# Interleaved attention and expert choice: two projection halves cut into quarters, and the probability masks issued earlier on VectorE

## What is computed

```
h = rmsnorm(x) * (1 + scale) + shift
q, k, v = split(h @ w_qkv + b_qkv)                 # 16 query heads, 4 key heads, width 64
p = softmax(scores + relative bias, with a sink)   # window of 128 keys, blocks of 128 tokens
x = x + g_m * (p @ v @ w_o + b_o)                  # the second projection
h2 = rmsnorm(x) * (1 + scale_f) + shift_f
top_val, top_idx = top_k(h2 @ w_r + b_r, 4)        # choice of 4 of 32 experts
x = x + g_f * sum over chosen experts of gate * (swiglu(h2 @ w_in[e]) @ w_out[e])
out = rmsnorm(x)
```

## Time and profile before

| what | value |
|---|---|
| median of 3 runs | 1975.12 us (1974.99 to 1975.28) |
| profiled execution, its own time | 1975.76 us |
| its span, first to last instruction | 1974.3 us |
| mean granted TensorE clock | 0.993 of full |
| TensorE busy | 1928.8 us (98%) |
| VectorE busy | 654.8 us (33%) |
| ScalarE busy | 467.3 us (24%) |
| GpSimd busy | 217.4 us (11%) |
| second projection, TensorE (line 1502) | 256 instructions, 114.1 us |

### The profile page before, as it was taken

How to read it: one execution, slowest core, us unless ns; L and a number is a source line. 1 busy time by engine, 2 the same in 40 slices (tenths; PEclk the granted TensorE clock), 3 DMA queues, 4 the chain that set the end, 5 groups by cost and what they waited for, 6 DMA issues and landing times.

```text
span 1974.3 us, 50841 instructions
## 1 busy us (share of the span) xinstructions
PE 1928.8 (98%) x22939; PEld 1729.2 (88%) x22939; DVE 654.8 (33%) x1886; ACT 467.3 (24%) x1382; POOL 217.4 (11%) x250
## 2 busy tenths in 40 slices
PE   7999999988999999999999999999999999999997
PEld 4756755445999999999999999999999999999997
DVE  2645766565422222131222222222222222222224
ACT  3104544441121211111111111121211111112213
POOL 2003000001011011010111111111010101101002
PEclk9999999989999999999999999999999999999999
DMA  9880121114988888888888787979797999999986
GB/s 359 308 173 21 43 75 54 43 43 158 372 312 298 289 302 315 300 290 302 310 293 324 290 324 287 338 272 358 259 368 253 354 321 327 345 328 339 323 322 223
DMA packets 150208, 523.95 MB, mean 265 GB/s; under 512 B 10027, under 2 KB 15811, under 8 KB 149987
## 3 DMA queue, kind: packets, MB, share of 16 engines
q1 hardware_dynamic: 131186, 467.68, 65.8%
q0 software_dynamic: 17200, 52.59, 7.8%
q10 hardware_dynamic: 1600, 0.36, 0.1%
HBM read 485.34 MB, written 34.21 MB: 263 GB/s over the span
## 4 chain that ended last, share of the span: by engine, by line
PE 94%; DVE 2%; DMA 1%; SPq 1%; issue 1%; POOL 0%; ACT 0%; ACTq 0%; DVEq 0%; POOLq 0%
PE ps L1654 47%; PE ps L1688 24%; PE ps L1502 5%; PE ps L1451 4%; PE ps L1510 3%; PE ps L1642 2%; PE ps L1628 2%; PE ps L1429 2%; PE ps L1483 1%; PE ps L1447 1%; DMA ring<-in_w_qkv 1%; PE ps L1472 1%; SPq L417 0%; SPq L405 0%; DMA U<-xn_d,U 0%
## 5 line engine op out<-in xcount | busy, mean ns | idle before, releaser
L1654 PE MATMUL ps<-U,ring 128*64 128x120 f32 (+11 forms) x13312 | 935.4, 270 | 2.2 <-DMA ring<-in_moe_w 1.7
L1654 PEld LDWEIGHTS ps<-U,ring 128*64 128x64 f32 (+1 forms) x13312 | 922.9, 149 | 10.1 <-issue 8.5
L1688 PE MATMUL ps<-U,ring 128*64 128x120 f32 (+11 forms) x6656 | 469.3, 270 | 2.1 <-issue 1.7
L1688 PEld LDWEIGHTS ps<-U,ring 128*64 128x64 f32 (+1 forms) x6656 | 461.6, 149 | 6.7 <-issue 6.0
L1238 DVE TENSOR_SCALAR U<-ps,U 128x120 f32<-128x120 f32 (+11 forms) x256 | 90.8, 355 | 1092.4 <-PE ps L1654 1092.4
L816 ACT ACTIVATE U<-U 128x120 f32<-128x120 f32 (+11 forms) x256 | 80.2, 313 | 889.1 <-DVE U L1238 889.1
L827 ACT ACTIVATE U<-ps,U,modT 128x120 f32<-128x120 f32 (+11 forms) x256 | 118.8, 464 | 290.0 <-PE ps L1688 289.9
L580 POOL DMA_INDIRECT acc_d<-U x43 | 43.2, 1006 | 767.1 <-DVE U L1230 763.4
L1502 PE MATMUL ps<-ring 128*128 128x512 f32 x256 | 114.1, 599 | 0.0
L1502 PEld LDWEIGHTS ps<-ring 128*128 128x128 f32 x256 | 47.3, 190 | 59.2 <-issue 59.2
L802 ACT ACTIVATE U<-ps,modT,Af 128x120 f32<-128x120 f32 (+11 forms) x252 | 91.6, 468 | 10.0 <-PE ps L1628 10.0
(11 more groups left out here) (229 smaller groups left out, 1107.1 us busy)
## 6 DMA issues: line engine op xcount, KB each, us to landing
ring<-in_moe_w SPq DMA_DIRECT2D x191, 2048.0 KB, 9.7
U<-in_w_mod SPq DMA_DIRECT2D x8, 2048.0 KB, 13.1
ring<-in_w_mod SPq DMA_DIRECT2D x3, 2048.0 KB, 19.7
ring<-in_w_qkv SPq DMA_DIRECT2D x3, 2048.0 KB, 18.0
acc_d<-xr SPq DMA_DIRECT2D x10, 512.0 KB, 2.9
xr<-in_x SPq DMA_DIRECT2D x8, 512.0 KB, 9.5
ring<-in_w_o SPq DMA_DIRECT2D x2, 2048.0 KB, 8.4
xn_d<-U SPq DMA_DIRECT2D x8, 512.0 KB, 2.6
```

The costliest lines, as they stand in the source:

```text
L1654: last = pe.matmul(bank(j % 4)[lo:hi, s * 256:s * 256 + n], w[:, k, s, (j % 2) * P + lo:(j % 2) * P + hi], xT[:, k, 0:n], start=(k == 0), ...
L1688: last = pe.matmul(bank(m % 4)[lo:hi, 0:n], w[:, k, (m % 4) * P + lo:(m % 4) * P + hi], actT[:, k, 0:n], start=(k == 0), stop=(k == KT - 1))
```

## The change

The second projection of a tile whose follower starts more than two steps later runs in three parts in three steps: columns 0 to 511, 512 to 767 and 768 to 1023. These are tiles 5 and 6, counted from 0 (steps 26, 27, 28 and 29, 30, 31). Parts are numbered through from 0 to 17 and their banks alternate by that number; the last one still uses its own bank. Gates, residuals and the waits of ScalarE and SyncE count parts instead of halves. On VectorE, in the steps 19, 21 and 23 to 31, `probs_out(u)` is issued in step u, behind the places and ahead of the denominators of u+1 and of everything that waits for norm, list or logits; before, it was the first of step u+1.

```diff
@@ -331,7 +331,15 @@
             return max(2 * KT + 2 * t, 4 * (t + 1) + 1)
 
         q_late = {n: (n // 2, n % 2) for n in range(2 * KT)}
-        o_half = {o_start(t) + h: (t, h) for t in range(TT) for h in range(2)}
+        o_parts = []
+        for t in range(TT):
+            o_parts.append((o_start(t), t, 0, 512))
+            if t + 1 < TT and o_start(t + 1) > o_start(t) + 2:
+                o_parts += [(o_start(t) + 1, t, 512, 768), (o_start(t) + 2, t, 768, D)]
+            else:
+                o_parts.append((o_start(t) + 1, t, 512, D))
+        o_at = {part[0]: n for n, part in enumerate(o_parts)}
+        parts_to = [sum(part[1] <= t for part in o_parts) for t in range(TT)]
         normed = {o_start(t) + 3: t for t in range(TT)}
         x2_half = {o_start(t) + 4 + h: (t, h) for t in range(TT) for h in range(2) if (t, h) != (TT - 1, 1)}
         logit_at = {o_start(t) + 6: t for t in range(TT - 1)}
@@ -339,7 +347,7 @@
         rank_at = {o_start(t) + 7: t for t in range(TT)}
         place_at = {o_start(t) + 8: t for t in range(TT)}
         STEPS = o_start(TT - 1) + 10
-        summed_after = {u + 1: u for u in range(UNITS) if u and (u in choose_at or u in place_at or u in normed)}
+        waits_late = {u for u in range(1, UNITS) if u in choose_at or u in place_at or u in normed}
 
         def lists_before(t):
             return sum(u < o_start(t) + 6 for u in place_at)
@@ -353,8 +361,8 @@
         def choice_bank(t):
             return bank(0) if t == LAST else bank(3)
 
-        def o_bank(t, h):
-            return bank(1) if (t, h) == (LAST, 1) else bank(7 - 2 * h)
+        def o_bank(n):
+            return bank(1) if n == len(o_parts) - 1 else bank(7 - 2 * (n % 2))
 
         def q_bank(n):
             return bank(7 - 2 * (n % 2))
@@ -450,10 +458,10 @@
                 sp.dma_start(xn_d[t * P:(t + 1) * P, :], xn2[:, t % 2, :]).then_inc(s_xnd[t % 2], 16)
 
             def store_x1(t):
-                sp.wait_ge(s_x1, 2 * t + 2)
+                sp.wait_ge(s_x1, parts_to[t])
                 sp.dma_start(acc_d[t * P:(t + 1) * P, :], xr[:, t, :]).then_inc(s_x1d, 16)
 
-            sp.wait_ge(s_x1, 2)
+            sp.wait_ge(s_x1, parts_to[0])
             for b in range(2):
                 sp.dma_start(acc_d[SEQ + b * P:SEQ + (b + 1) * P, :], xr[:, 0, :]).then_inc(s_x1d, 16)
             for t in range(TT - 2):
@@ -754,7 +762,7 @@
                                bank(6)[:, 0:256].rearrange("p (m n) -> p m n", m=2), ACT.Copy).then_inc(s_at, 1)
 
             def squares2(t):
-                act.wait_ge(s_x1, 2 * t + 2)
+                act.wait_ge(s_x1, parts_to[t])
                 if t:
                     act.wait_ge(s_sq2, t)
                 act.activation(junk2, xr[:, t, :], ACT.Square, accum_out=ss[:, TT + t:TT + t + 1]).then_inc(s_sq2, 1)
@@ -1012,18 +1020,18 @@
                 link(dve.tensor_tensor(out=den[:, u % 2, :], in0=rs[:, u % 2, :], in1=es[:, u % 2, :], op=ALU.add))
                 dve.reciprocal(rec[:, u % 2, :], den[:, u % 2, :]).then_inc(s_rec, 1)
 
-            def o_gate(t, h):
-                cols = slice(h * 512, h * 512 + 512)
-                dve.wait_ge(s_op, 2 * t + h + 1)
-                if t or h:
-                    dve.wait_ge(s_x1, 2 * t + h)
-                dve.tensor_tensor(out=gated, in0=o_bank(t, h), in1=gmB[:, cols], op=ALU.mult).then_inc(s_gt, 1)
-
-            def residual(t, h):
-                cols = slice(h * 512, h * 512 + 512)
-                dve.wait_ge(s_gt, 2 * t + h + 1)
+            def o_gate(n):
+                _, t, lo, hi = o_parts[n]
+                dve.wait_ge(s_op, n + 1)
+                if n:
+                    dve.wait_ge(s_x1, n)
+                dve.tensor_tensor(out=gated[:, 0:hi - lo], in0=o_bank(n)[:, 0:hi - lo], in1=gmB[:, lo:hi], op=ALU.mult).then_inc(s_gt, 1)
+
+            def residual(n):
+                _, t, lo, hi = o_parts[n]
+                dve.wait_ge(s_gt, n + 1)
                 dve.wait_ge(s_xb, t + 1)
-                dve.tensor_tensor(out=xr[:, t, cols], in0=xr[:, t, cols], in1=gated, op=ALU.add).then_inc(s_x1, 1)
+                dve.tensor_tensor(out=xr[:, t, lo:hi], in0=xr[:, t, lo:hi], in1=gated[:, 0:hi - lo], op=ALU.add).then_inc(s_x1, 1)
 
             def norm2(t):
                 dve.wait_ge(s_rstd2, t + 1)
@@ -1094,19 +1102,21 @@
 
             scores_in(0)
             for u in range(STEPS):
-                if 1 <= u <= UNITS:
+                if 1 <= u <= UNITS and u - 1 not in waits_late:
                     probs_out(u - 1)
-                if u < UNITS and u not in summed_after:
+                if u < UNITS and u - 1 not in waits_late:
                     denominators(u)
                 if u + 1 < UNITS:
                     scores_in(u + 1)
-                if u - 1 in o_half:
-                    o_gate(*o_half[u - 1])
-                    residual(*o_half[u - 1])
+                if u - 1 in o_at:
+                    o_gate(o_at[u - 1])
+                    residual(o_at[u - 1])
                 if u in place_at:
                     places(place_at[u])
-                if u + 1 < UNITS and u + 1 in summed_after:
-                    denominators(u + 1)
+                if u in waits_late:
+                    probs_out(u)
+                    if u + 1 < UNITS:
+                        denominators(u + 1)
                 if u in normed and normed[u] == LAST:
                     link(dve.tensor_scalar(in_group, e_f[:, 0:4], float(E), p_e[:, 0:1], ALU.mult, ALU.add))
                     link(dve.tensor_scalar(in_group, in_group, p_f[:, 0:1], None, ALU.is_equal))
@@ -1488,18 +1498,19 @@
             pe.wait_ge(s_qv, len(by_dve))
             pe.wait_ge(s_gB, 1)
 
-            def o_product(t, h):
+            def o_product(n):
+                _, t, lo, hi = o_parts[n]
                 if t == 0:
-                    pe.wait_ge(s_wo[h], 16)
+                    pe.wait_ge(s_wo[lo // 512], 16)
                 pe.wait_ge(s_at, 4 * t + 4)
-                if (t, h) == (LAST, 1):
+                if n == len(o_parts) - 1:
                     pe.wait_ge(s_sadd, UNITS)
-                elif t:
-                    pe.wait_ge(s_gt, 2 * t if t == LAST else 2 * t + h - 1)
-                else:
+                elif n >= 2:
+                    pe.wait_ge(s_gt, n if t == LAST else n - 1)
+                elif n == 0:
                     pe.wait_ge(s_qa, len(by_act) + 2 * KT)
                 for k in range(KT):
-                    last = pe.matmul(o_bank(t, h), attnT[:, k, t * P:(t + 1) * P], wo[:, k, h * 512:h * 512 + 512],
+                    last = pe.matmul(o_bank(n)[:, 0:hi - lo], attnT[:, k, t * P:(t + 1) * P], wo[:, k, lo:hi],
                                      start=(k == 0), stop=(k == KT - 1))
                 last.then_inc(s_op, 1)
 
@@ -1568,8 +1579,8 @@
                     scores_product(u + 2)
                 if u in q_late:
                     q_product(*q_late[u])
-                if u in o_half:
-                    o_product(*o_half[u])
+                if u in o_at:
+                    o_product(o_at[u])
                 if u in x2_half:
                     xn2_transpose(*x2_half[u])
                     if x2_half[u] == (LAST, 0):
```

## The result

Six runs of the changed kernel give a median of 1965.7 us (1962.83 to 1966.79), six of the kernel before 1975.2 (1970.83 to 1975.6): 9.5 us less, a ratio of 0.995 with a 95% interval of 0.9939 to 0.9961. The profiled execution took 1963.66 us with a span of 1962.2, so 12.1 us less in the span than the profiled execution before.

The account below looks back on a forecast made before the run. TensorE, 94% of the path, bounds the kernel; only its idle or low-clock time can be won. Idle 11.5 goes, 5.9 comes, 0.4 for quarters, 7.7 clock and tails: 12.9, less 1.7 spell; 1975.1 - 11.1 = 1964.0 us, range 1961.5 to 1969.0.

Parts of the forecast that it names:

- The walk: Steps 25 to 32 at full clock, both parts: last tile's first product starts at 426.8, not 439.7 us.
- the four waits of 1.9 us: TensorE's waits for masks before the probability transposes of steps 25, 27, 29, 31: 4 x 1.89 us would go.
- the new wait before the ranks of step 27: TensorE, after the first quarter product, waits 2.9 us for the choice's expert mask from VectorE.
- the chain from scores-in to the expert mask: VectorE, start of scores-in to finished expert mask: stays 9.1 us with the masks moved.
- the gain of 11.2: Whole kernel: 12.9 us earlier last-tile start less 1.7 us for one spell at the lower clock.
- The quarters' price: Two quarter products cost 7.2 us against 6.97 on TensorE; VectorE 0.8 us per quarter's gate and residual.
- Rival B: Only the masks pay; splitting moves the wait from step 28 to 27: gain about 8, so 1967 us; chance 0.12.
- the 7.7 us: Rest of the stage's gain, given to low clock and tails at idle stretches; bounded by 7.4 us.
- The 12.9: Start of the last tile's first product in step 33: 12.9 us earlier, 426.8 instead of 439.7.
- the spell after the change: TensorE after step 27's new wait: one lower-clock spell of 3.5 us, 1.7 lost; ends none and three of 5 us.
- the rival that the short steps stay at 1.2 GHz: Steps 28 to middle of 30 stay at low clock after step 27's wait: slower, 1984 us; chance 0.03.
- Rival C: VectorE, steps 19 to 29: masks ahead of each norm cost some 9 us, gain 2, 1973 us; chance 0.06.

Follow-up runs that it names:

- e7: Changed kernel with the choice issued ahead of the norm on VectorE: 1978.04 us against 1993.78 for the kernel before, ratio 0.9931.
- e5: The changed kernel again, unedited, on another chip: 1983.97 us against 1993.78 for the kernel before, ratio 0.9963.
- e3: Changed kernel with only the seventh tile split, masks still early: 1984.54 us against 1993.31 for the kernel before, ratio 0.9958.
- e11: Changed kernel with only the sixth tile split, masks still early: 1991.19 us against 1995.69 for the kernel before, ratio 0.9979.
- e1: Changed kernel with early masks alone, no tile split: 1987.43 us against 1993.31 for the kernel before, ratio 0.9978.
- e6: Kernel before with two unused matmuls behind the list products of steps 24, 26, 28, 30: 1996.87 us against 1993.78 unfilled, ratio 1.0014.
- e9: The kernel of e6 once more, on another chip: 1997.85 us against 1995.5 for the kernel before, ratio 1.001.
- e8: The kernel before again, unedited, on another chip: 1995.93 us against 1995.5 beside it, ratio 1.0003.
- e10: The kernel of e7 with eight unused matmuls ahead of the first expert slot: 1981.25 us against 1995.5 for the kernel before, ratio 0.9939.
- e4: Changed kernel, choice ahead of the norm and, in step 30, denominators ahead of masks: 1980.47 us against 1993.31 for the kernel before, ratio 0.9934.

## Why the prediction was right

**The walk.** It said that the last tile's first product follows the first list product (357.09) by 69.7 us with a full clock; the profiled execution took 69.8. Step by step, the four waits of 1.9 us went; 0.3 us were to stay before the scores of steps 25 and 27 (measured 0.2: 358.82 against 357.60 + 1.02); the new wait before the ranks of step 27 was put at 2.9 and is 2.68; that of step 31 at 1.2 and is 1.11; that of step 32 at 1.0 and is 0.87; the logits of step 28 wait no more. The claim that the chain from scores-in to the expert mask stays 9.1 us holds (379.86 to 389.0), and e7 shows its cause, the choice queued behind the norm and its wait for the root. Two slips in the sums change nothing: the new waits listed add to 6.0 and not 5.9, and the gain of 11.2 became 11.1 in the last line. That the profiled execution came out at 69.8 is in part luck, since it had no spell in the stage; e5 had one and took 71.4. The quarters' price was right: 3.72 us, and on VectorE 0.42 for a gate against the 0.40 taken from another operation.

**Attribution.** Rival B, that only the masks pay and the split just moves the wait from step 28 to 27, is true of the sixth tile (e3 against e5, e11 against e1) and false of the seventh (e3 against e1: 2.9 us in the medians on one chip, 2.8 in the stages with a full clock). The walk had this in its figures, since steps 30 and 31 lost waits there, but the prediction's text never said which tile carried the split's worth.

**The clock.** Two of its terms were off. The first is the 7.7 us that the sum gives to the low clock and tails of the kernel before, with half of TensorE's work in the spells, 7.4, as its bound. The spells cost 4.1 of the 12.8 us, and the waits 8.7 (82.6 to 78.5 to 69.8): with a full clock further waits show, as e6 has them, 0.33 before the transposes of step 30, 0.56 before the ranks of step 31 and 1.24 before the value product behind them, where the profile of before has none, none and 0.49. The 12.9 was not touched by this, because it is the measured start less the walked one and the 7.7 only its remainder.

The second is the spell after the change, in place more than in size. I took one, 1.7 us, behind the wait of step 27. The first profile has none there and one at the start of the slots, which the prediction had moving as a block; the second (e5) has both. Where nothing takes it up, a spell costs about half of TensorE's busy time in it: 3.4 us at 388 to 392 in e5, which cost its stage 1.6 against the first profile. The runs on the first chip spread over 4 us, from 1962.83 to 1966.79, which is some two such spells, and their median lies 1.7 us above the forecast of 1964.0. That fits one spell more than I counted, in part the slots' own. This is argued and not shown, and the mean clocks of those runs speak against it rather than for it: the fastest (1962.83) has the lowest, 0.995, and the slowest (1966.79) 0.997. The Trainium skill (TensorE: Matmul & The Clock Gate, what is actually happening) states that the throttle's judgement is free-running. The traces agree, in e5 against the first profile, in e6 against e9 and in e8 against the profile before: the same waits, but spells in other places and of other sums (0 and 3.4 us, 3.1 and 11.8, 17.1 and 10.3). I had weighed it down because three runs lay within 0.3 us; with six they lay within 4.8.

**Slower.** The spell of step 27 ended within 3.4 us in e5, so the rival that the short steps stay at 1.2 GHz had nothing for it. Rival C's price, the masks in front of the norm, is zero as argued: in step 27 VectorE still waits 0.95 us for the root after masks and denominators, and before the norms of steps 21 to 29 it waits 0.95 to 1.57 us; that of step 19 has no wait before the change either.

## What to carry to other kernels

Where one engine stands still for work queued behind another engine's wait, walk both queues step by step with the durations of the trace: the walk gives not only what goes but the next wait, and here it hit each to 0.25 us. Then look at what stands behind that next wait in program order; taking the choice out from behind the norm's wait, an edit of three lines, won 5.9 us in the medians (e7 against e5) where the split had won 3.9 (e5 against e1, with intervals that overlap); in the stages with a full clock it is 2.4 and 2.1. Do not price a spell at the lower clock by the work in it alone: look first for a wait behind it that would take it up. Cutting work to fill a later wait pays only where the shortened step has slack of its own.

## What the runs showed that I had not expected

The time at the lower clock varies with nothing else changed: 17.1 and 10.3 us in two profiles of the kernel before, 0 and 3.4 in two of the changed one. A wait of 1 to 3 us may or may not be followed by a spell of 3.4 us or more, and that spell cost up to 2.7 us (e3, 6.8 us at the lower clock) or nothing, by what waits stood behind it. e8, e10 and e11 also had spells between 20 and 60 us, far ahead of the stage, which the other profiles do not have; their first list products start at 358.5 to 360.8 against 355.9 to 357.2 us. The three profiles with 2.7 us of idle TensorE in the stage (e4, e7, e10) had none of it; with 5.1 (the changed kernel) it was 0 and 3.4, with 4.8 (e3) 6.8, so the sum of idle time alone does not decide. Filling waits with unused matmuls brought nothing in the time. The kernel before is slower by 18 to 20.5 us on the four chips of the experiments, and nearly all of it lies in the expert slots (1508.1 against 1488.7 us) at a granted clock of 1.00. Four chips agree to 2.4 us and one result stands alone, so whether the chip is the cause stays open.
